# Scaling a normed block by rows before it is transposed, with the work split over DVE and ACT

## The chip, the cores and the metric

The kernel runs on one core of a Trainium2 chip. TensorE is called PE here, VectorE DVE, ScalarE ACT, GpSimd POOL, SyncE SP. The metric is the time on the device in microseconds (us), median of several runs; lower is better.

## The reference

Two blocks of a network follow each other on 1024 tokens of width 1024, all in float32. The first ends with a mixture of 16 experts, whose rows are added back to the stream, and a norm with the gain `final_g`. The second begins with a norm, a scale and a shift per channel, and a wide product:

```python
x = x + expert_choice_ffn(h2, w_router, w_gate, w_up, w_down)   # end of the first block
x = rms_norm(x, final_g)
...
mod = jax.nn.silu(c) @ w_mod + b_mod                            # second block
shift, scale, gate = jnp.split(mod[:, None, :], 3, axis=-1)
h = rms_norm_2(x, g_pre) * (1 + scale) + shift
proj = h @ w_in                                                 # q, k, v, gates, recurrence
```

Both norms divide a row (a token) by the root of its mean square, so together they are one factor per token, worked out from the sum of squares of x and that of x times `final_g`. Scale and shift are per channel.

## The kernel before

Every engine runs a program of its own in the order written, and they wait for each other's counters only where the code says so (`wait_ge`). A matmul of float32 numbers is done as three: each operand is split into a high part (rounded to the reduced format fp32r) and the rest, the low part, and `three` (L442) multiplies high by high, high by low and low by high. A weight tile is rounded by ACT (`act_round_w`) and its low part made by DVE (`dve_low_w`).

The change lies in the passage from the experts to the attention of the second block. The 8 tiles of 128 tokens each are in `b_x1[i]`, with tokens on the partitions. The products need channels on the partitions, in `b_hid` (high, low), 8 tiles `kk` of 128 channels by two halves of 512 tokens. For each token tile i:

- `pe_place` (L2166) places the last expert's rows with four matmuls into two PSUM banks (`PLACE_BANKS`), two halves of the width.
- `dve_add_placed` (L2181) adds both to `b_x1[i]` and multiplies by the gain `final_g` into `b_t[i]`; this ends in the counter `b_gained`. SP stores `b_t[i]` to DRAM for later (`sp_store_t`).
- `act_square_rows` squares `b_x1[i]` (which = 0) and `b_t[i]` (which = 1) and sums each row. The squares themselves are not used: they go into `b_junk`.

For each half of four token tiles, `dve_scale` (L2215) works out the factor per token in column 7 of `stat`, with one square root on ACT. In the kernel before it then makes four diagonal matrices of it, PE multiplies them with ones (`pe_spread_scales`), and ACT copies the result to `b_rows`, in which every partition holds the 512 factors of the tokens. Meanwhile PE turns (transposes) the unscaled `b_t` (`pe_turn_second`), four blocks of 128 x 128 to a bank. For each kk, DVE multiplies the bank by the channel's scale and by `b_rows` into `b_tmp`, ACT adds the shift and rounds into the high part of `b_hid`, and DVE makes the low part (`dve_turn_second`, `act_turn_second`). There are three `b_tmp`.

The order on PE (`pe_second`, L2288): places of tiles 0 to 3; turns of the first half, kk 0 to 4; the spread; then the first head's q and k for the first half (`first_head`), six matmuls for each kk, with a turn behind kk 0 to 2 and with the places of tiles 4 to 7 behind kk 4, 6, 7 and 7; then values of head 0, the turns and the spread of the second half, values of head 1, and q and k of the second half. ACT's order: squares of tiles 0 to 3, the root, the spread, the turn of half 0, squares of 4 and 5, the evictions of q and k, squares of 6 and 7, root, and so on. DVE: adds of tiles 0 to 3, `dve_low_w` of weight tile 0, the scale, the turn of half 0, adds of 4 and 5, the rests of q and k, adds of 6 and 7, the scale and the turn of half 1. The values of head 0 go into the bank that held q of the first half, so they wait for its eviction.

Of the kernel before, what the change touches and what calls it, by code (L numbers as in the profile page):

```python
# [6 lines left out]
F32 = mybir.dt.float32  # L7
# [223 lines left out]
class Tiles:  # L231
# [141 lines left out]
    def second(self):  # L373
# [9 lines left out]
        self.b_diag = sb("b_diag", self.CONST + 936, [128, 4, 128])  # L383
        self.b_rows = sb("b_rows", y + 21568, [128, 512])
        self.b_tmp = [sb(f"b_tmp{i}", z + at, [128, 512]) for i, at in enumerate((5120, 5632, 8192))]
        self.b_junk = sb("b_junk", z + 10200, [128, 2, 1024])
# [49 lines left out]
def then(e):  # L436

    e.wait_ge(*e.last())
    return e
# [41 lines left out]
    return shaped(high[s][:, 0:size], k), shaped(low[s][:, 0:size], k)  # L481


def pe_channels(e, t, b, w, cols, hid, half, n_k, key, ready=None):

    tok = slice(512 * half, 512 * half + 512)
    e.wait_ge(*e.free(b))
    for kk in range(n_k):
        if ready:
            e.wait_ge(*e.at(*ready, kk))  # L490
        m = three(e, t.bank[b][:, :], [a[:, kk, cols] for a in w], [a[:, kk, tok] for a in hid],
                  kk == 0, kk == n_k - 1)
    m.then_inc(*e.fill(b, *key))


# [1597 lines left out]

TURN_BANKS = ((4, 5, 6, 7, 1, 4, 5, 6), (4, 5, 6, 7, 4, 5, 6, 7))
SCALE_BANK = 3

PLACE_BANKS = ((0, 1), (2, 3), (0, 1), (2, 3), (3, 7), (1, 4), (5, 6), (3, 7))


def pe_turn_second(e, t, half, kks):

    for j in range(4):
        e.wait_ge(*e.at("b_gained", 4 * half + j))
        for kk in kks:
            b = TURN_BANKS[half][kk]
            if j == 0:
                e.wait_ge(*e.free(b))
            m = e.transpose(t.bank[b][:, 128 * j:128 * j + 128], t.b_t[4 * half + j][:, 128 * kk:128 * kk + 128],  # L2110
                            t.k["ident"])
            if j == 3:
                m.then_inc(*e.fill(b, "b_turned", half, kk))


def pe_spread_scales(e, t, half):

    e.wait_ge(*e.free(SCALE_BANK))
    for j in range(4):
        e.wait_ge(*e.at("b_diag", half, j))  # L2120
        m = e.matmul(t.bank[SCALE_BANK][:, 128 * j:128 * j + 128], t.k["ones"], t.b_diag[:, j, :], start=True,
                     stop=True)
    m.then_inc(*e.fill(SCALE_BANK, "b_spread", half))


def act_spread_scales(e, t, half):
    e.wait_ge(*e.at("b_spread", half))
    if half:
        e.wait_ge(*e.at("b_scaled", 0, 7))
    e.activation(t.b_rows[:, :], t.bank[SCALE_BANK][:, :], ACT.Copy).then_inc(*e.evict(SCALE_BANK, "b_rows", half))  # L2130


def tmp_free(e, half, kk):
# [4 lines left out]
        e.wait_ge(*e.at("b_hid", 0, max(i for i in range(8) if i % 3 == kk)))  # L2138


def act_turn_second(e, t, half):
    for kk in range(8):
        e.wait_ge(*e.at("b_scaled", half, kk))
        e.activation(t.b_hid[0][:, kk, 512 * half:512 * half + 512], t.b_tmp[kk % 3][:, :], ACT.Identity,
                     bias=t.shift2[:, kk:kk + 1]).then_inc(*e.inc("b_high", half, kk))


def dve_turn_second(e, t, half):
    cols = slice(512 * half, 512 * half + 512)
    for kk in range(9):  # L2150
        if kk < 8:
            b = TURN_BANKS[half][kk]
            e.wait_ge(*e.at("b_rows", half))
            e.wait_ge(*e.at("b_turned", half, kk))
            tmp_free(e, half, kk)
            e.scalar_tensor_tensor(t.b_tmp[kk % 3][:, :], t.bank[b][:, :], t.scale2[:, kk:kk + 1],
                                   t.b_rows[:, :], ALU.mult, ALU.mult).then_inc(*e.evict(b, "b_scaled", half, kk))
        if kk:
            i = kk - 1
            e.wait_ge(*e.at("b_high", half, i))  # L2160
            e.scalar_tensor_tensor(t.b_hid[1][:, i, cols], t.b_tmp[i % 3][:, :], t.shift2[:, i:i + 1],  # L2161
                                   t.b_hid[0][:, i, cols].bitcast(F32), ALU.add,
                                   ALU.subtract).then_inc(*e.inc("b_hid", half, i))


def pe_place(e, t, i, part):  # L2166
# [32 lines left out]
def act_square_rows(e, t, i, which, before):  # L2199

    e.wait_ge(*e.at("b_gained", i) if which else e.at("b_added", i, 1))
    if before is not None:
        e.wait_ge(*e.at("b_squared", before, which))
    e.wait_ge(*e.at("last_made", 1))
    e.activation(t.b_junk[:, which, :], (t.b_x1, t.b_t)[which][i][:, :], ACT.Square,
                 accum_out=t.stat[:, which, i:i + 1]).then_inc(*e.inc("b_squared", i, which))


# [6 lines left out]
def dve_scale(e, t, half):  # L2215
    cols = slice(4 * half, 4 * half + 4)
    at = lambda n: t.stat[:, n, cols]
    e.wait_ge(*e.at("b_squared", 4 * half + 3, 0))
    e.wait_ge(*e.at("b_squared", 4 * half + 3, 1))
    e.tensor_scalar(at(2), at(0), 1.0 / D, EPS, ALU.mult, ALU.add).then_inc(*e.step())  # L2220
    e.tensor_scalar(at(3), at(1), 1.0 / D, None, ALU.mult).then_inc(*e.step())
    then(e).scalar_tensor_tensor(at(3), at(2), EPS, at(3), ALU.mult, ALU.add).then_inc(*e.inc("b_mean", half))
    dve_rsqrt(e, *(at(n) for n in range(3, 8)), ("b_root", half))
    then(e)
    if half:
        e.wait_ge(*e.at("b_spread", 0))
    for j in range(4):
        i = 4 * half + j
        e.tensor_scalar(t.b_diag[:, j, :], t.k["ident"], t.stat[:, 7, i:i + 1], None,
                        ALU.mult).then_inc(*e.inc("b_diag", half, j))  # L2230


def attention_units():
# [54 lines left out]
def pe_second(e, t):  # L2288
# [3 lines left out]
    for i in (2, 3):  # L2292
        for part in range(2):
            pe_place(e, t, i, part)
    pe_turn_second(e, t, 0, range(4))
    pe_turn_second(e, t, 0, (4,))
    pe_spread_scales(e, t, 0)

    def first_head(half, behind):

# [11 lines left out]
            behind(kk)  # L2312

    def behind_first(kk):
        if kk < 3:
            pe_turn_second(e, t, 0, (kk + 5,))
        for i, at in ((4, 4), (5, 6), (6, 7), (7, 7)):
            if at == kk:
                pe_place(e, t, i, 0)
                pe_place(e, t, i, 1)  # L2320

    def behind_second(kk):
        if kk < 4:
            pe_turn_second(e, t, 1, (kk + 4,))

    def scores(n):
        g = n // 4
# [47 lines left out]
    for u, steps in attention_units():  # L2375
        tile, first, last = unit_tile(u)
        wt = w_tile(t.b_wh, t.b_wl, tile % 2, 8)
        if u == ("values", 1, 0):
            pe_turn_second(e, t, 1, range(4))
            pe_spread_scales(e, t, 1)  # L2380
        e.wait_ge(*e.at("w_split", tile))
        if u[:2] == ("qk", 0):
            if u[3] == 0:
                first_head(u[2], behind_second if u[2] else behind_first)
        elif u[0] == "qk":
            n, half, which = u[1:]
            pe_channels(e, t, 2 * which + half, wt, slice(128 * which, 128 * which + 128), t.b_hid, half, 8,
                        ("qk", n, which, half), ("b_hid", half))
        elif u[0] == "values":
            n, half = u[1:]  # L2390
            pe_channels(e, t, value_banks(n)[0][half], wt, slice(128 * (n % 2), 128 * (n % 2) + 128), t.b_hid, half, 8,
                        ("v", n, half))
# [16 lines left out]


def act_second(e, t):
    def squares(first, last):
        for i in range(first, last):
            for which in range(2):
                act_square_rows(e, t, i, which, i - 1 if i else None)

    squares(0, 4)
    act_scale_root(e, t, 0)
    act_spread_scales(e, t, 0)
    act_turn_second(e, t, 0)  # L2420
    squares(4, 6)

    def exps(n):
        blocks = blocks_of(n // 4)
# [46 lines left out]
    for u, steps in attention_units():  # L2471
# [1 line left out]
        if u == ("qk", 0, 0, 0):  # L2473
            e.wait_ge(*e.at("b_t_out0", 3))
        if u == ("values", 0, 0):
            squares(6, 8)
            act_scale_root(e, t, 1)
        if u == ("qk", 0, 1, 0):
            act_spread_scales(e, t, 1)
            act_turn_second(e, t, 1)  # L2480
# [61 lines left out]
def dve_second(e, t):  # L2542
    for i in range(4):
        dve_add_placed(e, t, i)
    dve_low_w(e, t, 0)
    dve_scale(e, t, 0)
    dve_turn_second(e, t, 0)
    dve_add_placed(e, t, 4)
    dve_add_placed(e, t, 5)
    st = t.stat  # L2550

    def maxima(n):
# [47 lines left out]
    for u, steps in attention_units():  # L2600
# [3 lines left out]
        if u == ("values", 0, 0):  # L2604
            dve_add_placed(e, t, 6)
            dve_add_placed(e, t, 7)
            dve_scale(e, t, 1)
            dve_turn_second(e, t, 1)
# [814 lines left out]
```

## Time and profile before

| | us |
|---|---|
| median of 3 runs | 2859.09 (2859.02 to 2859.87) |
| the profiled execution | 2858.93 |
| its span in the trace | 2856.8 |
| PE busy | 2774.4 (97%) |
| DVE busy | 1840.4 (64%) |
| ACT busy | 1500.5 (53%) |
| PE, mean granted clock | 0.988 of full speed |

Times in the trace count from the start of the span. The passage described above lies between 1695 and 1765 us. "PEld" is the weight load of PE, which overlaps its matmuls. In a timeline a row is a start, a duration, the engine, the line, the operation, output and inputs, shape and count, and in brackets the idle time before it with what ended it. The matmuls of consecutive rows overlap, so the spacing of starts is what one costs.

### The profile page before, as it was taken

How to read it: one execution, taken by the hardware profiler on the slowest of the kernel's cores; microseconds unless marked ns; L12 is line 12 of the kernel's file. 1: busy time of each engine (PE TensorE's matmuls, PEld its weight loads, DVE VectorE, ACT ScalarE, POOL GpSimd, SP SyncE). 2: the span in 40 equal slices, each digit the busy share in tenths (PEclk: the TensorE clock that was granted, in tenths of full speed). 3: DMA queues.
4: the chain of work that ended last, by engine and by line, in shares of the span. 5: the costliest groups of instructions: out<-in, count | busy, mean ns of one | idle time of the engine just before them, and what ended most of it. 6: DMA issues, size and time to landing. Idle time of an engine off the chain costs nothing.

```text
span 2856.8 us, 33192 instructions
## 1 busy us (share of the span) xinstructions
PE 2774.4 (97%) x13616; PEld 2324.3 (81%) x13616; DVE 1840.4 (64%) x2051; ACT 1500.5 (53%) x1600; POOL 136.4 (5%) x81
## 2 busy tenths in 40 slices
PE   8999999869999999999999988999999999999998
PEld 6889988658888888888888867888888888888887
DVE  7563467778888888888888886333332356544344
ACT  5322322247777777777777775333333389743121
POOL 0211000110000000000000000000000011100000
PEclk9999999879999999999999999999999999999999
DMA  6222157779999999999999951111212211243332
GB/s 199 88 74 78 70 177 264 279 292 383 385 386 388 387 381 385 387 387 383 390 380 389 373 189 74 60 44 39 60 60 60 69 48 62 97 158 130 111 133 89
DMA packets 137126, 598.93 MB, mean 210 GB/s; under 512 B 17936, under 2 KB 39824, under 8 KB 80528
## 3 DMA queue, kind: packets, MB, share of 16 engines
q1 hardware_dynamic: 132080, 580.10, 54.3%
q0 software_dynamic: 4464, 16.25, 2.2%
q8 instruction: 107, 1.75, 0.2%
q10 hardware_dynamic: 432, 0.47, 0.1%
q14 instruction: 43, 0.35, 0.0%
HBM read 543.06 MB, written 52.53 MB: 208 GB/s over the span
## 4 chain that ended last, share of the span: by engine, by line
PE 95%; DVE 3%; issue 1%; ACT 1%; DMA 0%; SPq 0%; DVEq 0%; ACTq 0%
PE bank L444 25%; PE bank L446 25%; PE bank L445 25%; PE bank L1821 12%; PE bank L452 3%; PE bank L2370 1%; PE bank L770 0%; PE bank L1396 0%; PE bank L2726 0%; DVE r_sc L1614 0%; DVE r_at L1615 0%; DVE r_best L1611 0%; DVE b_x L2187 0%; PE bank L2371 0%; PE bank L830 0%
## 5 line engine op out<-in xcount | busy, mean ns | idle before, releaser
L1780 DVE TENSOR_TENSOR e_wl<-e_raw,e_wh 128x2048 fp32r<-128x2048 f32 x381 | 870.8, 2291 | 126.9 <-ACT e_wh L1772 126.3
L1772 ACT ACTIVATE e_wh<-e_raw 128x2048 fp32r<-128x2048 f32 x384 | 735.8, 1919 | 188.1 <-PE bank L446 107.6
L444 PE MATMUL bank<-b_hid_h,b_wh 128*128 128x512 f32 x1152 | 454.4, 394 | 6.6 <-DVE b_hid_l L2161 3.1
L446 PE MATMUL bank<-b_hid_h,b_wl 128*128 128x512 f32 x1152 | 449.5, 390 | 0.0
L445 PE MATMUL bank<-b_hid_l,b_wh 128*128 128x512 f32 x1152 | 449.0, 390 | 0.0
L444 PE MATMUL bank<-e_wh,e_xh 128*128 128x512 f32 x1024 | 406.1, 397 | 1.5 <-issue 1.5
L446 PE MATMUL bank<-e_wh,e_xl 128*128 128x512 f32 x1024 | 400.7, 391 | 0.0
L445 PE MATMUL bank<-e_wl,e_xh 128*128 128x512 f32 x1024 | 399.6, 390 | 0.0
L444 PEld LDWEIGHTS bank<-b_hid_h,b_wh 128*128 128x128 f32 x1152 | 216.7, 188 | 53.6 <-issue 7.6
L446 PEld LDWEIGHTS bank<-b_hid_h,b_wl 128*128 128x128 f32 x1152 | 216.5, 188 | 45.9
L445 PEld LDWEIGHTS bank<-b_hid_l,b_wh 128*128 128x128 f32 x1152 | 216.8, 188 | 43.0
L446 PEld LDWEIGHTS bank<-e_wh,e_xl 128*128 128x128 f32 x1024 | 192.9, 188 | 41.4
L444 PEld LDWEIGHTS bank<-e_wh,e_xh 128*128 128x128 f32 x1024 | 193.0, 188 | 39.8 <-issue 1.8
L445 PEld LDWEIGHTS bank<-e_wl,e_xh 128*128 128x128 f32 x1024 | 193.2, 189 | 38.5
L1821 PE MATMUL bank<-e_wh,e_hh 128*128 128x512 f32 x512 | 159.2, 392 | 1.4 <-DVE e_hl L1927 1.4
L1821 PE MATMUL bank<-e_wl,e_hh 128*128 128x512 f32 x512 | 157.8, 389 | 0.0
L1821 PE MATMUL bank<-e_wh,e_hl 128*128 128x512 f32 x512 | 157.8, 389 | 0.0
L444 PE MATMUL bank<-a_hid_h,a_wh 128*128 128x512 f32 x288 | 114.4, 397 | 0.0
L1821 PEld LDWEIGHTS bank<-e_wh,e_hl 128*128 128x128 f32 x512 | 96.1, 188 | 20.1
L1821 PEld LDWEIGHTS bank<-e_wl,e_hh 128*128 128x128 f32 x512 | 96.1, 188 | 20.1
L446 PE MATMUL bank<-a_hid_h,a_wl 128*128 128x512 f32 x288 | 112.3, 390 | 0.0
L445 PE MATMUL bank<-a_hid_l,a_wh 128*128 128x512 f32 x288 | 112.2, 389 | 0.0
(479 smaller groups left out, 4278.4 us busy)
## 6 DMA issues: line engine op xcount, KB each, us to landing
e_raw<-in_e_gate_dram SPq DMA_DIRECT2D x128, 1024.0 KB, 7.4
e_raw<-in_e_up_dram SPq DMA_DIRECT2D x128, 1024.0 KB, 7.5
e_raw<-in_e_down_dram SPq DMA_DIRECT2D x128, 1024.0 KB, 7.9
b_raw<-in_w_dram SPq DMA_DIRECT2D x36, 1024.0 KB, 5.8
a_raw<-in_w_dram SPq DMA_DIRECT2D x12, 1024.0 KB, 5.5
a_mod_w<-in_w_mod_dram SPq DMA_DIRECT2D x48, 256.0 KB, 4.4
a_x<-in_x_dram SPq DMA_DIRECT2D x16, 512.0 KB, 5.1
scr_sig<-a_sig SPq DMA_DIRECT2D x32, 256.0 KB, 2.5
```

Source lines behind the costliest of these rows:

```text
L444: e.matmul(out, a[0], b[0], start=first, stop=False)
L445: e.matmul(out, a[0], b[1], start=False, stop=False)
L446: return e.matmul(out, a[1], b[0], start=False, stop=last)
L452: m = e.transpose(t.bank[b][:, 128 * j:128 * j + 128], tile, t.k["ident"])
L1772: e.activation(t.e_wh[s][:, 0:2048], t.e_raw[slot][:, 0:2048], ACT.Copy).then_inc(*e.inc("e_round", i))
L1780: e.tensor_tensor(t.e_wl[s][:, 0:2048], t.e_raw[slot][:, 0:2048], t.e_wh[s][:, 0:2048].bitcast(F32), ALU.subtract).then_inc(*e.inc("e_spli ...
L1821: m = e.matmul(t.bank[4 + half][:, :], a[h][:, kk, :], wt[q][:, jj, 512 * half:512 * half + 512], start=(fq == 0 and kk == 0 and n == 0), ...
L2370: e.matmul(t.bank[b][:, at:at + 256], high, v, start=(j, i) == own[0], stop=False)
```

## The change

The rows are scaled while the tokens are on the partitions, before they are turned. `dve_scale` scales token tiles 0 and 1 of a half, ACT's new `act_scale` tiles 2 and 3, into new tiles `b_s`. PE turns `b_s` instead of `b_t`, and must wait for both scalings. The spread, the diagonals and `b_rows` are gone. Scale and shift of a channel are now one operation out of the bank: ACT does it for even kk, DVE for odd kk; ACT then copies into the high part for every kk, and DVE subtracts for the low part. The order changes too: `dve_low_w` comes behind `dve_scale`; turns 4 to 7 come behind kk 0 to 3 of the products; the places of tiles 4 and 5 come behind kk 2 and 4; DVE adds tiles 4 and 5 behind its kk 5 and 7, ACT squares tile 4 behind its kk 4 and 6, and tile 5 with 6 and 7; the first four turns of the second half come behind kk 3 of the second value unit. `b_junk` is gone: squares are written into `b_s[i]` or over `b_x1[i]`, for which the first square of tiles 4 to 7 now waits for `b_gained` too.

```diff
+        self.b_s = [sb(f"b_s{i}", z + 10200 + 1024 * i, [128, 1024]) for i in range(4)] + self.b_x1[4:8]
...
-def pe_channels(e, t, b, w, cols, hid, half, n_k, key, ready=None):
+def pe_channels(e, t, b, w, cols, hid, half, n_k, key, ready=None, behind=None):
...
+        if behind and kk < n_k - 1:
+            behind(kk)
...
+PLACE_BANKS = ((0, 1), (2, 3), (0, 1), (2, 3), (1, 3), (1, 3), (1, 3), (4, 5))
+def turn_bank(kk):
+    return 4 + kk % 4
+def pe_turn_second(e, t, half, kk):
+    b = turn_bank(kk)
+    e.wait_ge(*e.at("b_scaled", half))
+    e.wait_ge(*e.at("b_scaled_act", half))
+    e.wait_ge(*e.free(b))
+    four_transposes(e, t, b, [t.b_s[4 * half + j][:, 128 * kk:128 * kk + 128] for j in range(4)]
+                    ).then_inc(*e.fill(b, "b_turned", half, kk))
...
+def act_turn_second(e, t, half, behind):
     cols = slice(512 * half, 512 * half + 512)
     for kk in range(9):
+        if kk < 8 and kk % 2 == 0:
+            b = turn_bank(kk)
             e.wait_ge(*e.at("b_turned", half, kk))
             tmp_free(e, half, kk)
+            e.activation(t.b_tmp[kk % 3][:, :], t.bank[b][:, :], ACT.Identity, scale=t.scale2[:, kk:kk + 1],
+                         bias=t.shift2[:, kk:kk + 1]).then_inc(*e.evict(b, "b_shifted", half, kk))
+        if kk > 0:
+            e.wait_ge(*e.at("b_shifted", half, kk - 1))
+            e.activation(t.b_hid[0][:, kk - 1, cols], t.b_tmp[(kk - 1) % 3][:, :],
+                         ACT.Copy).then_inc(*e.inc("b_high", half, kk - 1))
+        behind(kk)
+
+def dve_turn_second(e, t, half, behind):
+    cols = slice(512 * half, 512 * half + 512)
+    for kk in range(10):
+        if kk < 8 and kk % 2:
+            b = turn_bank(kk)
+            e.wait_ge(*e.at("b_turned", half, kk))
+            tmp_free(e, half, kk)
+            e.tensor_scalar(t.b_tmp[kk % 3][:, :], t.bank[b][:, :], t.scale2[:, kk:kk + 1], t.shift2[:, kk:kk + 1],
+                            ALU.mult, ALU.add).then_inc(*e.evict(b, "b_shifted", half, kk))
+        if kk > 1:
+            e.wait_ge(*e.at("b_high", half, kk - 2))
+            e.tensor_tensor(t.b_hid[1][:, kk - 2, cols], t.b_tmp[(kk - 2) % 3][:, :],
+                            t.b_hid[0][:, kk - 2, cols].bitcast(F32),
+                            ALU.subtract).then_inc(*e.inc("b_hid", half, kk - 2))
+        behind(kk)
...
+def act_square_rows(e, t, i, which):
+    if which or i >= 4:
+        e.wait_ge(*e.at("b_gained", i))
+        if which:
+            e.wait_ge(*e.at("b_squared", i, 0))
+        out = t.b_x1[i]
+    else:
+        e.wait_ge(*e.at("b_added", i, 1))
+        e.wait_ge(*e.at("e_split", last_expert_tile(14)))
+        out = t.b_s[i]
...
+    for i in range(4 * half, 4 * half + 2):
+        e.tensor_scalar(t.b_s[i][:, :], t.b_t[i][:, :], t.stat[:, 7, i:i + 1], None, ALU.mult).then_inc(*e.step())
+    e.mark("b_scaled", half)
+
+def act_scale(e, t, half):
+    e.wait_ge(*e.at("b_rsqrt", half))
+    for i in range(4 * half + 2, 4 * half + 4):
+        e.activation(t.b_s[i][:, :], t.b_t[i][:, :], ACT.Copy, scale=t.stat[:, 7, i:i + 1]).then_inc(*e.step())
+    e.mark("b_scaled_act", half)
...
 def pe_second(e, t):
+    for kk in range(4):
+        pe_turn_second(e, t, 0, kk)
...
     def behind_first(kk):
+        if kk < 4:
+            pe_turn_second(e, t, 0, kk + 4)
+        for i, at in ((4, 2), (5, 4), (6, 7), (7, 7)):
             if at == kk:
                 pe_place(e, t, i, 0)
                 pe_place(e, t, i, 1)
+    def behind_values(kk):
+        if kk == 3:
+            for i in range(4):
+                pe_turn_second(e, t, 1, i)
...
 def act_second(e, t):
+    def behind_first(kk):
+        if kk in (4, 6):
+            act_square_rows(e, t, 4, kk // 2 - 2)
+    squares(0, 1, 2, 3)
     act_scale_root(e, t, 0)
+    act_scale(e, t, 0)
+    act_turn_second(e, t, 0, behind_first)
...
 def dve_second(e, t):
+    dve_scale(e, t, 0)
     dve_low_w(e, t, 0)
+    def behind_first(kk):
+        if kk in (5, 7):
+            dve_add_placed(e, t, (kk + 3) // 2)
+    dve_turn_second(e, t, 0, behind_first)
```

## Rows read from the trace of the kernel before

**Rows 1.** The page: the chain by engine, and one DMA issue

```profile
PE 95%; DVE 3%; issue 1%; ACT 1%; DMA 0%; SPq 0%; DVEq 0%; ACTq 0%
...
b_raw<-in_w_dram SPq DMA_DIRECT2D x36, 1024.0 KB, 5.8
```

**Rows 2.** Waits of PE, 1700 to 2200: who waited for whom, us in total, times, longest

```profile
PE bank L2110 <- DVE b_t L2190: 3.6, 2, 1.8
PE bank L2121 <- DVE b_diag L2229: 3.2, 2, 2.0
PE bank L444 <- DVE b_hid_l L2161: 3.1, 1, 3.1
PE bank L444 <- DVE t_q L2620: 2.4, 2, 1.7
```

**Rows 3.** Windows of 1 us: busy us of PE, PEld, DVE, ACT, POOL; granted clock, DMA share, GB/s

```profile
1707.00:1708.00 1.00, 0.07 (x1) 0.07 (x2) 1.00 (x2) 0.89 (x3) 0.00 (x0) 0.50 0.55 221
...
1720.00:1721.00 1.00, 1.00 (x6) 0.96 (x6) 1.00 (x3) 0.72 (x1) 0.00 (x0) 0.69 0.00 0
```

**Rows 4.** Timeline of PE, 1700 to 1770: start, us, instruction, idle before

```profile
1717.09 0.77 PE L444 MATMUL bank<-b_hid_h,b_wh 128*128 128x512 f32 x1 [3.11 <-DVE b_hid_l L2161]
...
1727.04 0.62 PE L2176 MATMUL bank<-e_last_h,e_places 128*128 128x512 f32 x2
...
1736.61 0.50 PE L444 MATMUL bank<-b_hid_h,b_wh 128*128 128x512 f32 x1 [1.70 <-DVE t_q L2620]
...
1742.21 1.91 PE L2110 MATMUL bank<-cst,b_t 128*128 128x128 f32 x16
...
1746.19 0.48 PE L444 MATMUL bank<-b_hid_h,b_wh 128*128 128x512 f32 x1
```

**Rows 5.** Timeline of DVE, the same stretch

```profile
1710.00 0.16 DVE L2220 TENSOR_SCALAR stat<-stat 128x4 f32<-128x4 f32 x1
...
1711.50 0.87 DVE L2229 TENSOR_SCALAR b_diag<-cst,stat 128x128 f32<-128x128 f32 x4
...
1727.92 1.29 DVE L2187 TENSOR_TENSOR b_x<-bank,b_x 128x512 f32<-128x512 f32 x2 [1.13 <-PE bank L2176]
1729.24 1.23 DVE L2190 TENSOR_TENSOR b_t<-b_x,b_fg 128x1024 f32<-128x1024 f32 x1
```

**Rows 6.** Timeline of ACT, the same stretch

```profile
1708.88 0.18 ACT L2205 ACTIVATION_READ_ACCUMULATOR b_junk<-b_t 128x1 f32 x1
...
1764.72 0.60 ACT L2493 ACTIVATE t_k<-bank 128x512 fp32r<-128x512 f32 x1
1765.21 1.91 ACT L2063 ACTIVATE b_wh<-b_raw 128x2048 fp32r<-128x2048 f32 x1
```

**Rows 7.** Groups by line and form, DVE and ACT: busy us, mean ns, idle before

```profile
L2620 DVE TENSOR_TENSOR t_q<-bank,t_q 128x512 fp32r<-128x512 f32 x24 | 16.6, 691 | 70.8 <-ACT t_q L2493 70.8
...
L1135 DVE TENSOR_SCALAR a_x<-a_x,stat 128x1024 f32<-128x1024 f32 x5 | 3.5, 750 | 0.1
...
L995 ACT ACTIVATE a_hid_h<-bank,pc 128x512 fp32r<-128x512 f32 x16 | 10.8, 688 | 9.3 <-PE bank L452 9.2
...
L2857 ACT ACTIVATE m_bah<-m_g 128x512 fp32r<-128x512 f32 x8 | 5.1, 632 | 4.5 <-DVE m_g L2896 4.5
...
L1007 ACT ACTIVATE a_x<-a_x,stat 128x1024 f32<-128x1024 f32 x3 | 3.3, 1144 | 0.8 <-DVE stat L462 0.8
```

**Rows 8.** Timeline of PE in the opening of the kernel

```profile
13.96 3.60 PE L452 MATMUL bank<-cst,a_x 128*128 128x128 f32 x16 [13.96 <-DVE a_x L1135]
17.25 0.53 PE L444 MATMUL bank<-a_hid_h,a_wh 128*128 128x512 f32 x1
```

**Rows 9.** Timeline of PE at the first expert

```profile
601.82 0.77 PE L444 MATMUL bank<-e_wh,e_xh 128*128 128x512 f32 x1 [1.46 <-issue]
...
607.91 0.40 PE L446 MATMUL bank<-e_wh,e_xl 128*128 128x512 f32 x1
```

**Rows 10.** Timeline of ACT in the opening

```profile
15.14 1.48 ACT L995 ACTIVATE a_hid_h<-bank,pc 128x512 fp32r<-128x512 f32 x2 [1.27 <-PE bank L452]
```

More of the change, by code:

```diff
@@ L2092, in dve_begin_second @@
     dve_low_w(e, t, 1)
[L2096 to L2130, printed above, removed]
+PLACE_BANKS = ((0, 1), (2, 3), (0, 1), (2, 3), (1, 3), (1, 3), (1, 3), (4, 5))
[8 more added lines that the diff above has]
+                    ).then_inc(*e.fill(b, "b_turned", half, kk))
 def tmp_free(e, half, kk):
@@ L2138, in tmp_free @@
         e.wait_ge(*e.at("b_hid", 0, max(i for i in range(8) if i % 3 == kk)))
[L2141 to L2148, printed above, removed]
+def act_turn_second(e, t, half, behind):
     cols = slice(512 * half, 512 * half + 512)
@@ L2150, in dve_turn_second @@
     for kk in range(9):
-        if kk < 8:
-            b = TURN_BANKS[half][kk]
-            e.wait_ge(*e.at("b_rows", half))
+        if kk < 8 and kk % 2 == 0:
+            b = turn_bank(kk)
             e.wait_ge(*e.at("b_turned", half, kk))
             tmp_free(e, half, kk)
[L2156 to L2163, printed above, removed]
+            e.activation(t.b_tmp[kk % 3][:, :], t.bank[b][:, :], ACT.Identity, scale=t.scale2[:, kk:kk + 1],
+                         bias=t.shift2[:, kk:kk + 1]).then_inc(*e.evict(b, "b_shifted", half, kk))
@@ L2196, in sp_store_t @@
         e.dma_start(t.scr_t[128 * i:128 * i + 128, :], t.b_t[i][:, :]).then_inc(*e.dma(f"b_t_out{i // 4}", i))
[L2199 to L2205, printed above, removed]
+def act_square_rows(e, t, i, which):
[8 more added lines that the diff above has]
+        out = t.b_s[i]
+    e.activation(out[:, :], (t.b_x1, t.b_t)[which][i][:, :], ACT.Square,
                  accum_out=t.stat[:, which, i:i + 1]).then_inc(*e.inc("b_squared", i, which))
@@ L2223, in dve_scale @@
     dve_rsqrt(e, *(at(n) for n in range(3, 8)), ("b_root", half))
+    e.mark("b_rsqrt", half)
     then(e)
[L2225 to L2230, printed above, removed]
+    for i in range(4 * half, 4 * half + 2):
[6 more added lines that the diff above has]
+    e.mark("b_scaled_act", half)
 def attention_units():
@@ L2294, in pe_second @@
             pe_place(e, t, i, part)
-    pe_turn_second(e, t, 0, range(4))
-    pe_turn_second(e, t, 0, (4,))
-    pe_spread_scales(e, t, 0)
+    for kk in range(4):
+        pe_turn_second(e, t, 0, kk)
     def first_head(half, behind):
@@ L2377, in pe_second @@
         wt = w_tile(t.b_wh, t.b_wl, tile % 2, 8)
-        if u == ("values", 1, 0):
-            pe_turn_second(e, t, 1, range(4))
-            pe_spread_scales(e, t, 1)
         e.wait_ge(*e.at("w_split", tile))
@@ L2391, in pe_second @@
             pe_channels(e, t, value_banks(n)[0][half], wt, slice(128 * (n % 2), 128 * (n % 2) + 128), t.b_hid, half, 8,
-                        ("v", n, half))
+                        ("v", n, half), behind=behind_values if u == ("values", 1, 0) else None)
         else:
@@ L2411, in act_second, with squares @@
 def act_second(e, t):
-    def squares(first, last):
-        for i in range(first, last):
+    def squares(*tiles):
+        for i in tiles:
             for which in range(2):
-                act_square_rows(e, t, i, which, i - 1 if i else None)
-    squares(0, 4)
+                act_square_rows(e, t, i, which)
+    def behind_first(kk):
+        if kk in (4, 6):
+            act_square_rows(e, t, 4, kk // 2 - 2)
+    squares(0, 1, 2, 3)
     act_scale_root(e, t, 0)
-    act_spread_scales(e, t, 0)
-    act_turn_second(e, t, 0)
-    squares(4, 6)
+    act_scale(e, t, 0)
+    act_turn_second(e, t, 0, behind_first)
     def exps(n):
@@ L2475, in act_second @@
         if u == ("values", 0, 0):
-            squares(6, 8)
+            squares(5, 6, 7)
             act_scale_root(e, t, 1)
+            act_scale(e, t, 1)
         if u == ("qk", 0, 1, 0):
-            act_spread_scales(e, t, 1)
-            act_turn_second(e, t, 1)
+            act_turn_second(e, t, 1, lambda kk: None)
             e.activation(t.stat[:, 3, :], t.stat[:, 2, :], ACT.Sqrt).then_inc(*e.inc("r1_root"))
@@ L2607, in dve_second @@
             dve_scale(e, t, 1)
-            dve_turn_second(e, t, 1)
+            dve_turn_second(e, t, 1, lambda kk: None)
             dve_rsqrt(e, st[:, 2, :], st[:, 3, :], st[:, 4, :], st[:, 5, :], t.r1[:, :], ("r1_root",))
```

12 lines of the change are left out of this document (1 added, 11 removed).

## The prediction

> **What bounds the kernel now.** I read the page first: TensorE (PE) is busy 97% of the span, and the chain that ended last is 95% PE [rows 1]. So only time in which PE waits, or runs at its lower clock, can be won or lost. The waits of PE from 1700 us on, where the changed functions run, are then the stake: four groups of 12.3 us in sum [rows 2]. The slices of one microsecond show its second part: PE's granted clock is 0.50 (1.2 GHz, against 2.4 at 1.00) from 1707 on, after two waits of 1.8 us with a short piece of turns between, and comes back to 1.00 within the slice that begins at 1720, by its mean of 0.69 at about 1720.6 [rows 2, 3]. The timeline of PE gives the order: places, turns of the first half, a spread of the scales, the first product at 1717.09, so 3.5 us of it at the low clock. A value unit is 24 matmuls in 5.6 us (1736.61 to 1742.21), 0.23 us each, and a kk of the first head is 6 of them, 1.37 us [rows 4]. The first half's head ends with placed tiles at 1734.91; PE then waits 1.70 us for bank 0 [rows 4], because ACT squares tiles 4 and 5 before it evicts q. The first value unit starts at 1736.61, the turns of the second half at 1742.21, the second value unit at 1746.19.
>
> **Start of the first half.** Before, the chain is: squares end at 1709.07 (1708.88 and 0.18), the DVE is in `dve_low_w` until 1710.0, eight short operations lead to the first diagonal at 1711.50 [rows 5, 6], then PE spreads, ACT copies, and DVE, ACT, DVE make the first b_hid: product at 1717.09. After the change low_w comes behind the scaling, so the statistics start when the squares are in, at about 1709.2 (0.1 us for a signal, as between rows of different engines here). The 1.5 us from 1710.00 to 1711.50 then give the root at 1710.7. The scaling itself is not in this stretch, but the first block does just this: two tensor_scalar of 128x1024 at 0.75 us on DVE, ACT's copy with scale at 1.14 us [rows 7]. Two each: DVE done at 1712.1, ACT at 1712.9. PE can turn from 1713.0 on. The 16 turns before the first product took 3.3 us in the opening of the kernel (13.96 to 17.25) [rows 8] and 16 took 1.91 us warm, so 3.8 at half the clock [rows 4]; between 3.3 and 3.8 I take the first, an execution of this very form: PE is free at 1716.3. Beside it: ACT starts on bank 4 1.2 us after the first turn (as 15.14 after 13.96 [rows 8, 10]), at 1714.2, scale with shift 0.69 us (the PSUM eviction with a column operand), copy from SBUF 0.63 us, DVE's remainder 0.69 us [rows 7], with signals b_hid 0 at 1716.4. DVE's low_w, 2048 elements or twice the 1.23 us of 1024 [rows 5], runs 1712.1 to 1714.5 and is in nobody's way. First product 1716.5: 0.6 us earlier than before.
>
> **Supply of the first half.** A kk costs DVE half a shift out of the bank and a remainder. The shift as a tensor_scalar out of a bank has no row: half of the 0.75 for 1024 elements out of SBUF is the lower bound, the 0.69 of a tensor_tensor out of a bank the upper [rows 7]; I take 0.69, as it too reads the bank. That makes 1.0 us for a kk, and 0.97 on ACT, against PE's 1.37 and 0.44 for a turn between (4 of the 16 in 1.91 us [rows 4]): 1.81 us. Before, DVE had two operations for each kk. So up to kk 3 the products are fed in both kernels. The lighter load of DVE has no stall of PE to win here: PE waits for b_hid once, 3.1 us before the first product, and never after it [rows 2]. Turn 4 now comes between products: +0.4.
>
> **The inserted steps.** Here something is new. ACT's loop calls its square of tile 4 behind kk 4, before it copies tile kk 4 into b_hid. That square waits for `b_gained` of tile 4, which DVE makes behind its kk 5, out of banks that PE fills behind its kk 2. All of ACT's queue stands behind the wait, first the copy of kk 4, then DVE's remainder of it, then PE's product. Worked out from PE's end of kk 2: turn 6 0.44, DVE's add starts 0.88 after the places (1727.04 to 1727.92 [rows 4, 5]), add and gain 2.54 [rows 5], then ACT's square 1.15 with the reading of its sum [rows 6], copy 0.63, remainder 0.69, signals 0.2: 6.5 us. PE has in the meantime turn 6 0.44, place 4 0.91 (4 matmuls of 0.23), product 3 1.37, turn 7 0.44: 3.2 us. PE waits **3.3 us** before product 4. The same from the start of product 4: product 1.37, 0.88, add and gain of tile 5 on DVE 2.54, remainder 6 behind it 0.69, signals 0.15: 5.6 us, against product 4, place 5, product 5, 3.7 us: PE waits **1.9 us** before product 6. In the kernel before both adds stand behind the whole turn, so neither wait exists. In return the first q is evicted at once, since only tiles 5 to 7 are still to be squared: under places 6 and 7 (1.8 us) ACT's 0.60 and DVE's 0.69 fit, and the 1.70 us gap goes.
>
> **Second half.** Before: turns of 1.91 from 1742.21, then the wait for the diagonals and the spread, and the second value unit at 1746.19 [rows 4]: 2.07 us beside the turns. After, the turns come in the middle of the second value unit, 5.6 + 2.7 = 8.3 us after the first one's start, but ACT has more in front. Counted from the end of the head's last product: evictions of k on ACT and DVE 1.4, adds of tiles 6 and 7 2 x 2.5 [rows 5], then both squares of tile 7 one behind the other, as the first now waits for b_gained too, 2.5, statistics 1.5, ACT's two scalings 2.2, signals 0.1: 12.7 us. PE: places 6 and 7 1.8, and 8.3: 10.1. PE waits **2.6 us** inside the value unit. Against 2.07 removed: +0.6. The products of half 1 are then fed ahead of PE as before, and the second wait for q's rest, 0.7 us of the 2.4 [rows 2], stays.
>
> **What costs nothing.** The eight fewer spread matmuls per half are in the 2.07 and in the start. SP's store of a tile waits for its gain, at most some us later; weight tile 2 is issued behind the last store, which waits for tile 7's gain near 1742 in both kernels, and lands in 5.8 us, while ACT rounds it at 1765.21 [rows 1, 6]: some 17 us of cover, so the move does nothing; without it each us late would be one of PE. POOL has no part. The low part of weight tile 0 is 4.5 us later, still 2.0 us ahead of its product. Squares written into dead tiles instead of b_junk cost the same.
>
> **The clock.** PE is now idle from the last placed tile to 1713, and so cold at the first turn; the turns are done in one piece. From the rows: the matmuls after 1717.09 ran 3.5 us at the low clock (1.7 us lost) [rows 3, 4], those after 601.82 for 6.1 us, till they are 0.40 long and not 0.63 (3.0 lost) [rows 9]. For the new kernel the bounds are none lost (warm by the first product, as the opening's first product, 0.53 long, right after 3.3 us of turns [rows 8], where no record shows a clock that had been low) and 3.0. I take 1.7, between the two and what the kernel before lost: difference 0. The Trainium skill (TensorE: Matmul & The Clock Gate, section PE-mode transpose) says that transposes do not bring the full clock, since they do not count as work of PE in the same way. No row here can show it: the one long piece of turns behind an idle PE is the opening. By that rule the sum would be up to 1.3 higher, by the opening's rows 1.7 lower.
>
> **Sum.** Start -0.6, turn 4 +0.4, clock 0, wait at kk 4 +3.3, wait at kk 6 +1.9, gap -1.7, second half +0.6: **+3.9 us**. The profiled execution took 2858.93 us (the span of 2856.8 and 2.1 around it), the median of the runs is 2859.09, 0.16 above; the difference is put on the median: **2863.0 us**, +0.14%. What a measurement here can tell from no change is about 0.2%, 5.7 us: so this is no measurable change.
>
> **Rivals.**
> - *The clock falls in the new wait.* PE's 1.70 us gap left the warm pace as it was (the value unit behind it), two gaps of 1.80 close to each other took it away [rows 2 to 4]. 3.3 us of idleness lies between. If it falls, 3.4 to 6.1 us of matmuls run at half rate, 1.7 to 3.0 us more: 2864.7 to 2866.0, and to 2867.5 if the 2.6 us wait does it too. It decides for "slower" once the loss passes 1.8 us. For it: the wait is longer than any warm gap survived; against: work fills both sides. Chance 0.32.
> - *The turns warm nothing.* As above: low clock for up to 6.1 us from 1716.5, +1.3 on the forecast: 2864.3. For it: the clock came back 3.5 us after the first product and not earlier, though turns and a spread went before [rows 3, 4]; against: those were pieces with gaps. Chance 0.15. The Trainium skill's sentence on transposes, cited above, is this case.
> - *The turns warm PE fully.* Products start at 0.23 us: 1.7 less, 2861.3. Chance 0.13.
> - *ACT and DVE run ahead, no new wait.* Without the three waits the sum is -0.6 +0.4 -1.7 -2.07, so -3.9, and with the clock up -5.6: 2853.5 to 2855.2. For it: the lighter DVE load. Against: the wait for b_gained stands in the code, and PE's places for it come after kk 2. It becomes a gain only if ACT's square could start by 1722. Chance 0.05, of which 0.02 past -0.2%.
> - The forecast itself 0.35.
>
> **Numbers.** Slower by over 0.2%: 0.30, nearly all from the falling clock. Faster 0.02. Same 0.68. The range goes from the warm case less 1 us of error to the falling clock in both waits: 2860.0 to 2867.0.
>
> **What would show it.** In the profile after: turns from 1713.0 in one piece; first product near 1716.5; ACT's square of tile 4 idle for 6 us until DVE's b_t; PE's L444 waiting some 3.3 us on b_hid_l at kk 4 and 1.9 at kk 6; no wait on t_q before the first value unit; a wait of some 2.6 us for the turns inside the second; the clock in the windows after each wait. Wrong would be: a first product later than 1717, products of kk 1 to 3 starved, or a clock that stays down through the head.

## The result, and the profile after

| kernel | median, us | lowest to highest | runs |
|---|---|---|---|
| before | 2859.89 | 2858.45 to 2861.79 | 20 |
| changed | 2864.48 | 2862.74 to 2865.76 | 20 |

The ratio is 1.0015, with a 95% interval of 1.0008 to 1.0022: the change costs 4.6 us, between 2 and 6. That lies within the 0.2% set as the bound of no measurable change, but with 20 runs of each the interval no longer holds 1. The profiled execution took 2864.62 us with a span of 2862.8, 6.0 more than the span of before; that is more than 4.6 because the profiled execution of before lies 1.0 under its median and this one 0.1 above.

The 20 executions of the changed kernel lie in two groups: nine from 2862.74 to 2863.70 us with a mean granted clock of 0.986 to 0.988 (mean 0.9873), eleven from 2864.40 to 2865.76 with 0.985 to 0.987 (mean 0.9860). The profiled one is of the second group.

The waits of PE from 1700 us on, in the changed kernel (us in total, times, longest), against [rows 2]:

```profile
PE bank L450 <- ACT b_s L2227: 10.3, 1, 10.3
PE bank L442 <- DVE b_hid_l L2148: 3.8, 2, 3.0
PE bank L450 <- DVE b_x L2220: 2.6, 1, 2.6
...
PE bank L442 <- DVE t_q L2625: 0.7, 1, 0.7
```

The first is one wait of 10.3 us in place of several short ones around the early turns; it ends in an earlier first product, so it costs nothing by itself. Of the two waits for q's rest (2.4 us in [rows 2]) the one before the first value unit is gone; the 0.7 left is the later one. New are 3.8 us for b_hid in the middle of the first head and 2.6 us for the scaled rows of half 1.

The timeline of PE at these places:

```profile
1712.82 3.65 PE L450 MATMUL bank<-cst,b_s 128*128 128x128 f32 x16 [10.29 <-ACT b_s L2227]
1716.36 0.73 PE L442 MATMUL bank<-b_hid_h,b_wh 128*128 128x512 f32 x1
...
1724.50 0.60 PE L450 MATMUL bank<-cst,b_s 128*128 128x128 f32 x4
1728.13 0.80 PE L442 MATMUL bank<-b_hid_h,b_wh 128*128 128x512 f32 x1 [3.03 <-DVE b_hid_l L2148]
...
1730.85 1.06 PE L2164 MATMUL bank<-e_last_h,e_places 128*128 128x512 f32 x2
...
1735.58 0.50 PE L442 MATMUL bank<-b_hid_h,b_wh 128*128 128x512 f32 x1 [0.80 <-DVE b_hid_l L2148]
...
1740.23 0.39 PE L442 MATMUL bank<-b_hid_h,b_wh 128*128 128x512 f32 x1
...
1751.17 3.54 PE L450 MATMUL bank<-cst,b_x 128*128 128x128 f32 x16 [2.62 <-DVE b_x L2220]
1754.46 0.47 PE L442 MATMUL bank<-b_hid_h,b_wh 128*128 128x512 f32 x1
```

To be seen, against [rows 4]: the turns in one piece, the first product 0.7 us earlier, then 3.03 us of idleness before product 4 (the products of the first head are numbered by their kk). The matmuls after it are spaced 0.43 us, not 0.23 (two placed halves take 1.06, not 0.62). Another 0.80 us go before product 6. The first value unit starts at 1740.23 with no idle time ahead of it, 3.6 us later than in the kernel before. The turns of half 1 wait 2.62 us and then take 3.54, where 16 took 1.91 before; from their start to the next product it is 3.29.

What stood in front of product 4 is in ACT's and DVE's timelines, which answer to [rows 5] and [rows 6]:

```profile
1725.68 1.06 ACT L2198 ACTIVATE b_x<-b_x 128x1024 f32<-128x1024 f32 x1 [5.66 <-DVE b_t L2178]
...
1726.74 0.61 ACT L2132 ACTIVATE b_hid_h<-b_tmp 128x512 fp32r<-128x512 f32 x1
```

```profile
1723.10 1.29 DVE L2175 TENSOR_TENSOR b_x<-bank,b_x 128x512 f32<-128x512 f32 x2 [1.13 <-PE bank L2164]
1724.42 1.23 DVE L2178 TENSOR_TENSOR b_t<-b_x,b_fg 128x1024 f32<-128x1024 f32 x1
1727.38 0.69 DVE L2148 TENSOR_TENSOR b_hid_l<-b_tmp,b_hid_h 128x512 fp32r<-128x512 f32 x1 [1.73 <-ACT b_hid_h L2132]
```

ACT stands idle 5.66 us in front of its square of `b_x1[4]`, until DVE's gain of tile 4 (`b_t`, L2178) is done. The copy of kk 4 into b_hid comes behind it (1726.74), the low part on DVE at 1727.38, product 4 at 1728.13.

The clock, in windows of 1 us of the changed kernel (the granted clock is the third number from the end):

```profile
1716.00:1717.00 1.00, 1.00 (x5) 0.64 (x4) 0.70 (x2) 1.00 (x3) 0.00 (x0) 0.54 0.00 0
...
1727.00:1728.00 1.00, 0.00 (x0) 0.00 (x0) 0.62 (x1) 1.00 (x3) 0.00 (x0) 0.58 0.75 307
...
1733.00:1734.00 1.00, 1.00 (x4) 0.81 (x3) 0.96 (x3) 0.00 (x0) 0.00 (x0) 0.51 0.00 0
...
1751.00:1752.00 1.00, 0.83 (x4) 0.86 (x5) 0.00 (x0) 0.55 (x2) 0.00 (x0) 0.52 1.06 451
...
1754.00:1755.00 1.00, 1.00 (x6) 0.92 (x5) 0.81 (x2) 1.00 (x2) 0.00 (x0) 0.77 0.00 0
```

By the mean of a window the clock comes up at about 1716.9, 0.5 us after the first product, falls at 1727.2 inside the new wait, is back at 1734.0, falls again at 1751.0 at the end of the third wait, and is back at 1754.5.

### The profile page after: what moved, and what is told of

It is laid out like the page before. It is cut to its first block, busy times and chain, and to the rows that moved or that the text cites. A ratio compares the mean times of both kernels' runs of the same rounds, so it can differ in the third digit from the quotient of the medians.

```text
span 2862.8 us, 33145 instructions
## 1 busy us (share of the span) xinstructions
PE 2775.5 (97%) x13600; PEld 2324.8 (81%) x13600; DVE 1835.7 (64%) x2039; ACT 1507.0 (53%) x1610; POOL 136.3 (5%) x81
## 4 chain that ended last, share of the span: by engine, by line
PE 95%; DVE 3%; ACT 1%; issue 1%; DMA 0%; SPq 0%; ACTq 0%; DVEq 0%
PE bank L442 25%; PE bank L444 25%; PE bank L443 25%; PE bank L1821 12%; PE bank L450 4%; PE bank L2372 1%; PE bank L770 0%; PE bank L1396 0%; PE bank L2731 0%; DVE r_sc L1614 0%; DVE r_at L1615 0%; DVE b_x L2175 0%; DVE r_best L1611 0%; PE bank L2373 0%; PE bank L830 0%
```

## The experiments

Each was timed in 5 rounds with the kernel before beside it; in the first four its median was 2859.46, in the last four 2859.22. The interval of a ratio reaches some 2.6 us to either side, so a difference of 1 to 2 us between two rows is not clear by the intervals alone. Where it is read below it rests on the traces, and on the executions of the two kernels where their ranges do not overlap.

| what is changed | median, us | ratio to before (95%) |
|---|---|---|
| changed kernel, ACT squares tile 4 behind the turn | 2861.02 | 1.0005 (0.9996 to 1.0014) |
| changed kernel, later tiles in the order of before | 2857.15 | 0.9994 (0.9985 to 1.0003) |
| kernel before, with the inserted steps alone | 2863.62 | 1.0015 (1.0006 to 1.0024) |
| changed kernel, PE kept at work in its waits | 2861.85 | 1.0008 (0.9999 to 1.0017) |
| the second one, turns of half 1 behind kk 6 | 2855.23 | 0.9985 (0.9976 to 0.9994) |
| that one, squares that wait for the add alone | 2853.98 | 0.9981 (0.9972 to 0.9990) |
| kernel before, low part of the weight behind the scale | 2858.54 | 0.9995 (0.9986 to 1.0004) |
| the second one, tile 5 squared before q is evicted | 2860.20 | 1.0003 (0.9994 to 1.0012) |

**The square of tile 4 moved out of the turn.**

```diff
 def act_second(e, t):
-    act_turn_second(e, t, 0, behind_first)
+    act_turn_second(e, t, 0, lambda kk: None)
+    squares(4)
```

> The changed kernel with one thing moved: ACT squares tile 4 behind its whole turn of half 0, not behind its kk 4 and 6. Theory (inserted steps hold up the products): product 4 no longer waits for ACT's square and copy, only for DVE's add of tile 4 with the remainder behind it; the wait of 3.0 us shrinks to about 1.2 us, the clock does not fall there, and with both the first value unit starts 3 to 4 us earlier than in the changed kernel (1740.2); time about 1.5 to 3.5 us under the changed kernel's. Rival (the rows scaled first are what costs, through the late turns and ACT's load): the wait before product 4 stays near 3 us and the time stays within 1 us of the changed kernel's.

```profile
1713.29 3.34 PE L450 MATMUL bank<-cst,b_s 128*128 128x128 f32 x16 [10.28 <-ACT b_s L2227]
1716.83 0.47 PE L442 MATMUL bank<-b_hid_h,b_wh 128*128 128x512 f32 x1 [0.20 <-DVE b_hid_l L2148]
...
1726.48 0.50 PE L442 MATMUL bank<-b_hid_h,b_wh 128*128 128x512 f32 x1 [1.18 <-DVE b_hid_l L2148]
...
1732.05 0.50 PE L442 MATMUL bank<-b_hid_h,b_wh 128*128 128x512 f32 x1 [1.66 <-DVE b_hid_l L2148]
...
1747.69 1.94 PE L450 MATMUL bank<-cst,b_x 128*128 128x128 f32 x16 [2.61 <-DVE b_x L2220]
```

```profile
1716.00:1717.00 1.00, 0.81 (x6) 0.60 (x5) 0.89 (x3) 0.88 (x2) 0.00 (x0) 0.91 0.00 0
```

The wait before product 4 is 1.18 us, as expected for DVE's add alone. Product 6 waits 1.66, and the clock is not lost in either, nor in the wait of 2.61 before the turns of half 1. That is one execution, at 2859.72: three of the 11 lie from 2858.95 to 2859.72, all at a mean clock of 0.988, the other eight from 2860.78 to 2861.91 at 0.986 or 0.987. The first value unit starts at 1736.8. The median is 1.6 us above before, where the changed kernel's is 4.6 above: 3.0 us less. So of the 3 us before product 4, some 1.8 were ACT's square standing in the queue. Its window at 1716 also shows the clock coming back at 1716.2, ahead of the first product at 1716.83: in this execution nothing but turns had run since the idle time.

**All steps for the later tiles in the order of before.** The square as above, and:

```diff
-PLACE_BANKS = ((0, 1), (2, 3), (0, 1), (2, 3), (1, 3), (1, 3), (1, 3), (4, 5))
+PLACE_BANKS = ((0, 1), (2, 3), (0, 1), (2, 3), (1, 3), (4, 5), (6, 7), (1, 3))
...
-        for i, at in ((4, 2), (5, 4), (6, 7), (7, 7)):
+        for i, at in ((4, 4), (5, 6), (6, 7), (7, 7)):
...
 def dve_second(e, t):
-    dve_turn_second(e, t, 0, behind_first)
+    dve_turn_second(e, t, 0, lambda kk: None)
+    dve_add_placed(e, t, 4)
+    dve_add_placed(e, t, 5)
```

> The changed kernel with the order of before for the later tiles: places behind kk 4, 6, 7, 7, adds of tiles 4 and 5 and squares of tile 4 behind the whole turn of half 0. Theory: no wait of PE in the first head at all, clock at 1.00 from about 1717, head over near 1733, first value unit near 1733 to 1734 against 1740.2; the wait of some 2.6 us inside the second value unit stays, perhaps with a fall of the clock. Against before: start 0.6, clock 1.5, gap of q 1.7 won, second half 0.6 to 2.0 lost: 2 to 4 us faster than before. Rival (scaling by rows is what costs): slower than before by 2 us or more still.

```profile
PE bank L450 <- ACT b_s L2227: 9.8, 1, 9.8
PE bank L450 <- DVE b_x L2220: 3.3, 1, 3.3
```

```profile
1719.00:1720.00 1.00, 1.00 (x8) 0.83 (x7) 0.00 (x0) 0.17 (x1) 0.00 (x0) 0.96 0.00 0
...
1746.00:1747.00 1.00, 1.00 (x7) 1.00 (x8) 0.00 (x0) 0.66 (x2) 0.00 (x0) 0.70 0.97 410
...
1749.00:1750.00 1.00, 1.00 (x4) 0.82 (x4) 0.75 (x2) 1.00 (x3) 0.00 (x0) 0.60 0.00 0
```

No wait for b_hid is left in the list, and the first value unit starts at 1734.2, 6 us earlier than in the changed kernel. The wait for the scaled rows of half 1 stays and is 3.3 us. The clock fell at 1746.4, 0.4 us after that wait had ended (1745.96), and was back at 1749.8. The profiled execution is the slowest of the 11 (2859.61): six lie from 2856.33 to 2857.15, all at a mean clock of 0.988, five from 2858.36 to 2859.61 at 0.986 or 0.987. The same program thus varies by more than 2 us, and the slower executions are those with the lower clock. The median is 2.3 us under before, so 6.9 under the changed kernel by their distances to before; the interval against before still holds 1 (4.3 faster to 0.9 slower). The expectation of 2 to 4 us is met at its lower end, and the rival's 2 us or more of loss lies outside the interval. Scaling the rows first is thus not what made the kernel slower.

**The inserted steps alone, in the kernel before.** Places behind kk 2 and 4, and:

```diff
 def act_turn_second(e, t, half):
     for kk in range(8):
+        if half == 0 and kk in (4, 6):
+            act_square_rows(e, t, 4, kk // 2 - 2, 3)
...
 def dve_turn_second(e, t, half):
     ...
+        if half == 0 and kk in (4, 6):
+            dve_add_placed(e, t, 2 + kk // 2)
```

with the squares of tile 5 behind the eviction of q, as in the changed kernel.

> The kernel before with only the inserted steps: places of tiles 4 and 5 behind kk 2 and 4, adds on DVE and squares of tile 4 on ACT inside the turn of half 0 at the same spots, tile 5 squared with 6 and 7. The scaling stays as before. Theory: PE waits about 2.8 us before product 4 and 1.5 to 2 us before product 6, the 1.70 us gap before the first value unit goes: net 2 to 5 us slower than before, more if the clock falls in the wait. Rival: no wait appears, time within 1 us of before or faster.

```profile
1715.52 0.77 PE L444 MATMUL bank<-b_hid_h,b_wh 128*128 128x512 f32 x1 [3.11 <-DVE b_hid_l L2163]
...
1728.24 0.50 PE L444 MATMUL bank<-b_hid_h,b_wh 128*128 128x512 f32 x1 [2.34 <-DVE b_hid_l L2163]
...
1734.52 0.80 PE L444 MATMUL bank<-b_hid_h,b_wh 128*128 128x512 f32 x1 [2.38 <-DVE b_hid_l L2163]
```

PE waits 2.34 us before product 4 and 2.38 before product 6, where the kernel before waits for nothing; the wait for q's rest before the first value unit is gone, as in the changed kernel. The clock stayed through the first wait and fell in the second (it was low from 1734.2 to 1737.6). The cost is 4.2 us, almost the 4.6 of the whole change. The first wait was half a microsecond shorter than expected, the second half a microsecond longer.

**PE kept at work while it waits.** In `pe_turn_second` of the changed kernel:

```diff
+    if (half, kk) == (1, 0):
+        e.wait_ge(*e.free(b))
+        e.wait_ge(*e.at("b_gained", 7))
+        for _ in range(5):
+            four_transposes(e, t, b, [t.b_t[4][:, 128 * j:128 * j + 128] for j in range(4)])
     e.wait_ge(*e.at("b_scaled", half))
...
+    if (half, kk) == (0, 7):
+        for _ in range(5):
+            four_transposes(e, t, b, [t.b_s[j][:, 128 * kk:128 * kk + 128] for j in range(4)])
```

> The changed kernel with PE kept at work in its two long waits: the turn of kk 7 is done five more times into its own bank before the one that counts, and before the turns of half 1 tile 4 of b_t is turned five times into their first bank, which is then written over. Each adds 20 turns, about 2.2 us. Theory (the falls of the clock in the waits cost by themselves): product 4 starts at the same time, about 1728, the clock stays at 1.00, product 6 starts about 1.9 us earlier; the turns of half 1 take 1.9 and not 3.3 us; together some 3 us under the changed kernel. Rival (the fall of the clock is only a companion, all is hidden by the waits): time unchanged within 1 us.

```profile
1724.77 2.78 PE L450 MATMUL bank<-cst,b_s 128*128 128x128 f32 x24
1728.38 0.50 PE L442 MATMUL bank<-b_hid_h,b_wh 128*128 128x512 f32 x1 [0.83 <-DVE b_hid_l L2156]
...
1733.96 0.50 PE L442 MATMUL bank<-b_hid_h,b_wh 128*128 128x512 f32 x1 [1.66 <-DVE b_hid_l L2156]
...
1746.81 2.34 PE L450 MATMUL bank<-cst,b_t 128*128 128x128 f32 x20
1749.63 1.94 PE L450 MATMUL bank<-cst,b_x 128*128 128x128 f32 x16 [0.48 <-ACT b_x L2235]
```

Product 4 starts 16.1 us behind the first turn (1712.28 to 1728.38), against 15.3 in the changed kernel, whose clock came back sooner at the start (4.1 us behind the first turn, 5.9 here). From product 4 to product 6 it is 5.58 us, as worked out for a PE at the full clock, and 7.45 in the changed kernel. The 16 turns of half 1 take 1.94 us and not 3.54. No window of this stretch from 1719 on is under 1.00. Forty transposes more, and 2.2 us less (2.4 above before, not 4.6), a little less than the 3 us expected: the lost clock is a cost of its own. No execution here took more than 2862.20 us and none of the changed kernel less than 2862.74, but the intervals against before overlap, so that it is about half of the loss is an estimate. The 11 executions lie within 1.1 us of each other, without the second group that the changed kernel has.

**The turns of half 1 behind kk 6.** To the second run's kernel:

```diff
     def behind_values(kk):
-        if kk == 3:
+        if kk == 6:
```

> The second run's kernel (later tiles in the order of before) with the first four turns of half 1 behind kk 6 of the second value unit in place of kk 3. Theory: the chain on DVE and ACT to the scaled rows ends at the same time, PE has three kk or 2.05 us more to do before it needs them, so its wait falls from 3.3 to about 1.2 us, the clock stays up there, and the time is 2 to 3.5 us under the second run's, some 5 us under before. b_hid of half 1 is ready 3.1 us after the first turn, PE needs it after 3.3: no new wait. Rival (that wait is made up for later, at the gap before the next value unit): time within 1 us of the second run's.

```profile
1713.10 3.65 PE L450 MATMUL bank<-cst,b_s 128*128 128x128 f32 x16 [10.29 <-ACT b_s L2227]
...
1745.08 1.94 PE L450 MATMUL bank<-cst,b_x 128*128 128x128 f32 x16 [1.24 <-DVE b_x L2220]
...
1748.06 0.48 PE L442 MATMUL bank<-b_hid_h,b_wh 128*128 128x512 f32 x1 [0.34 <-DVE b_hid_l L2148]
```

The wait is 1.24 us, the clock stays, and the turns take 1.94. A small wait of 0.34 us for b_hid appears, which was not expected. The median is 4.0 us under before against 2.3 for the second run's kernel: 1.7 less, somewhat under the expectation, and the interval is now clear of before. Eight of the 11 executions lie from 2854.84 to 2855.55, the highest at 2856.66.

**Squares that wait for the add alone.** On top of it:

```diff
-    if which or i >= 4:
+    if which:
         e.wait_ge(*e.at("b_gained", i))
...
+    elif i >= 4:
+        e.wait_ge(*e.at("b_added", i, 1))
+        e.wait_ge(*e.at("b_turned", 0, 7))
+        out = t.b_s[i - 4]
```

> The run with the turns behind kk 6, and the squares of b_x1 of tiles 4 to 7 written into the scaled tiles of half 0, which are turned by then, so that they wait for the add only and not for the gain. Theory: ACT's last square ends about 1.2 us earlier and the remaining wait of some 1.2 us inside the second value unit goes to about 0: 1 to 1.5 us under the run with the turns behind kk 6. Rival (ACT's length and not its wait sets the chain): unchanged within 0.5 us.

```profile
PE bank L450 <- ACT b_s L2230: 9.8, 1, 9.8
...
PE bank L442 <- DVE b_hid_l L2148: 0.6, 2, 0.3
```

The wait for the scaled rows of half 1 is gone from the list. The median is 5.2 us under before, 1.2 under the last run's (2853.64 to 2854.25, all under the lowest there), and 9.8 under the changed kernel by their distances to before. This is the fastest version of the study.

**The low part of the weight behind the scale, alone.**

```diff
 def dve_second(e, t):
-    dve_low_w(e, t, 0)
     dve_scale(e, t, 0)
+    dve_low_w(e, t, 0)
```

> The kernel before with one thing moved: DVE makes the low part of weight tile 0 behind the scale of half 0. Theory (the earlier start comes from this move, not from the scaled rows): the statistics start 0.8 us earlier, first product near 1716.3 after an origin like that of before, 0.7 to 0.8 us earlier; time 0 to 1 us under before, less than can be told. Rival (the shorter path of the scaled rows gives the start): first product unchanged at 1717.1, since DVE's low part of 2.3 us now stands ahead of its first b_tmp.

```profile
1710.67 0.88 DVE L2229 TENSOR_SCALAR b_diag<-cst,stat 128x128 f32<-128x128 f32 x4
1711.46 2.29 DVE L2069 TENSOR_TENSOR b_wl<-b_raw,b_wh 128x2048 fp32r<-128x2048 f32 x1
1713.81 1.41 DVE L2156 SCALAR_TENSOR_TENSOR b_tmp<-bank,scale,b_rows 128x512 f32<-128x512 f32 x2
```

```profile
1716.25 0.77 PE L444 MATMUL bank<-b_hid_h,b_wh 128*128 128x512 f32 x1 [3.11 <-DVE b_hid_l L2161]
```

The first diagonal comes 0.83 us earlier, the low part of the weight ends just ahead of the first `b_tmp`, and the first product starts at 1716.25 against 1717.09. The passage begins at the same time in both (first placed tile at 1696.18 and 1696.19). The changed kernel's start at 1716.36, with a passage that begins 0.2 earlier, is no better, so this move is enough for the earlier start. The time, 0.7 us under before, can't be told from it; in this execution the clock came back at 1722.3, in that of before at 1720.6.

**Tile 5 squared before q is evicted.** To the second run's kernel:

```diff
-    squares(4)
+    squares(4, 5)
...
-            squares(5, 6, 7)
+            squares(6, 7)
```

> The second run's kernel with the squares of tile 5 back ahead of the eviction of q and k on ACT, as in the kernel before. Theory (the gap before the first value unit comes from them): the first value unit starts after a wait of 1.2 to 2 us for q's rest, which the second run did not have, and the later chain gets no shorter; time 0 to 2 us above the second run's, as part of the delay is taken out of the wait inside the second value unit. Rival (q's eviction is late for another reason): no wait there.

```profile
1733.81 1.06 ACT L2198 ACTIVATE b_x<-b_t 128x1024 f32<-128x1024 f32 x1
...
1734.86 0.58 ACT L2492 ACTIVATE t_q<-bank 128x512 fp32r<-128x512 f32 x1
```

```profile
1736.29 0.50 PE L442 MATMUL bank<-b_hid_h,b_wh 128*128 128x512 f32 x1 [2.88 <-DVE t_q L2620]
...
1748.01 2.95 PE L450 MATMUL bank<-cst,b_x 128*128 128x128 f32 x16 [3.27 <-DVE b_x L2220]
```

The eviction of q stands behind the square of tile 5, and the value unit waits 2.88 us for it, more than expected; the clock stays at 1.00 through this wait. The wait inside the second unit is 3.27 us, as it was: the whole chain slid, and nothing was taken out of it. The run is 1.0 us above before, so 3.3 above the second run's, where 0 to 2 was expected; that the later wait would absorb a part was wrong.

## Why the prediction was right

Forecast were 2863.0 us and 3.9 us more than before; measured were 2864.48 and 4.6. Term by term, by the profiled executions (whose spans differ by 6.0 us, with both falls of the clock in it; the passage begins 0.2 us earlier in the changed kernel's, so it costs 6.2):

| step | predicted | measured |
|---|---|---|
| start of the first product | -0.6 | -0.5 (-0.7, less 0.2 by which all ran earlier) |
| clock after it, against before | 0 | -1.4 (0.3 lost, not 1.7) |
| wait before product 4 | +3.3 | +3.0 |
| wait before product 6 | +1.9 | +0.8, and +3.0 since product 4: 2.7 by the clock, 0.3 by the stop itself |
| gap before the first value unit | -1.7 | -1.7 |
| turn 4 between the products | +0.4 | +0.4 |
| half 1: wait, turns, spread | +0.6 (wait 2.6; less 2.07 it is 0.5) | +1.9 (wait 2.62 and 3.29 for the turns, 3.98 in all before) |
| products of half 1 | 0 | +0.3 |

**The mechanism** was as described. The chain from kk 2 through place, add, gain, square, copy and remainder to product 4 is in the timelines link by link, and the first experiment cuts it at ACT, the second altogether. The third puts it into the kernel before and gets the loss back. The third wait has the size and the place predicted, and is shortened and removed by the fifth and sixth.

**The clock** is where the sum was put together wrongly, by terms of opposite sign, so that the sum came out within 1 us is in part luck. The forecast took it to stay up in the new waits, and gave its fall a chance of 0.32. In the profiled execution it fell in both long ones; behind the first, PE took 6.65 us from product 4 to its next wait where the filled kernel takes 3.92, a loss of 2.7 us that is near the upper bound of 3.0, and the second fall costs 1.6 (the turns of half 1 and their way to the next product 3.29, where the fifth experiment has 1.69). At the start the clock was taken to be away for 3.4 us of products as before, and it was away for 0.5. The rival with the falling clock named 2864.7 to 2867.5, and the measured median lies 0.2 under its low end; the better start alone would put it there. The fourth experiment shows that the fall costs by itself. How often the clock falls in the unprofiled executions is seen only by their mean clocks: the two groups of the changed kernel, and those of the second experiment, fit one fall more or less, but no trace of both groups of one kernel was kept.

**The wait before product 6** measured 0.8, not 1.9, since PE took 6.65 us, most of them at the low clock, for what had been counted as 3.7. When PE kept its clock, in the first and fourth experiments, the wait was 1.66.

**The rule on transposes** of the Trainium skill (TensorE: Matmul & The Clock Gate, section PE-mode transpose), that they don't count as work of PE in the same way and don't bring the full clock, does not hold for the float32 turns of this kernel. In the first experiment's window the clock is back at 1716.2, before the first product, with 16 turns since the idle time and nothing else. In the changed kernel it is back at 1754.5, when the turns of half 1 are just over. (The code calls a transpose with the identity; the trace names it MATMUL and shows no mode.) [rows 8] could have told: the opening's 16 turns take 3.29 us to the next product, exactly what those of half 1 take at a granted clock of 0.50, and the product behind them is 0.53 long. They ran at the low pace, and turns alone ended it, though the windows there say 1.00. The rival that rested on it (2864.3) names nearly the measured time and is wrong all the same: the time lost at the start was 0.3 us, not 3.0.

**What was over-optimistic:** the products of half 1 were said to be fed ahead of PE as before. They are, but for one:

```profile
1764.81 0.81 DVE L2144 TENSOR_SCALAR b_tmp<-bank,scale,shift 128x512 f32<-128x512 f32 x1 [1.65 <-PE bank L450]
1765.54 1.89 DVE L2148 TENSOR_TENSOR b_hid_l<-b_tmp,b_hid_h 128x512 fp32r<-128x512 f32 x3
```

DVE's low part of kk 5 stands in its queue behind the shift of kk 7, which waits for the last turn (1764.17). Product 5 starts at 1766.27, 0.50 us behind the matmul before it and not 0.23. The measured terms add up to 5.8 us with it; the other 0.4 of the 6.2 are spread over the passage.

## What to carry to other kernels

A step put into the loop of an in-order engine to use its idle time brings its own wait with it, and everything queued behind that wait is late: ask where the input of the inserted step comes from, count that chain from PE's own instruction, and put the step where its input is already there. An idle time of PE of 2.4 to 3.3 us can cost more than its length, as the clock may fall in it or just behind it, and the work behind it, which sets the next wait, runs at half rate. With the inserted steps elsewhere and the turns late enough the same idea runs 5.2 us under the kernel before; how much of that is the scaled rows themselves, and how much the order around them (q evicted ahead of tile 5's squares, the weight's low part behind the scale), was not taken apart.

## What had not been expected of the hardware

- Turns alone bring PE's clock back, 2.9 us after the first of them in the first experiment (1713.29 to 1716.2). The moment differs between executions: in the second experiment, the same code up to there, it was 6.0 us (1713.03 to 1719.1), the first products among them. By an estimate from these rows this alone moves the time by some 1.2 us (2.5 us of products at half rate, from 1716.56 on).
- A wait of PE of one length may or may not cost the clock. After 2.62 us it was lost in the changed kernel and after 2.61 us kept in the first experiment. Of the waits behind the first product, the shortest with a fall was 2.38 us (third experiment, before product 6), the longest without one 2.88 us (last experiment, before the first value unit).
- ACT's scale with shift out of a bank took 0.78 us, DVE's tensor_scalar with two columns out of a bank 0.81, above both of its bounds (0.38 and 0.69).
